# A hybrid attention and recurrent network: stick-breaking in head pairs, banded attention ahead of neighbourhood attention

## What is computed

```python
def stick_breaking_block(q_blk, k_ctx, v_ctx, q0):
    ...
    z = jnp.einsum('bthd,bshd->bhts', q_blk.astype(jnp.float32),
                   k_ctx.astype(jnp.float32)) * (SB_HEAD_DIM ** -0.5)
    before = jnp.arange(s_len)[None, :] < (q0 + jnp.arange(tq))[:, None]
    log_keep = jnp.where(before, jax.nn.log_sigmoid(-z), 0.0)
    csum = jnp.cumsum(log_keep, axis=-1)
    weights = jnp.where(before, jnp.exp(jax.nn.log_sigmoid(z) + csum[..., -1:] - csum), 0.0)
    return jnp.einsum('bhts,bshd->bthd', weights, v_ctx.astype(jnp.float32))

def stick_breaking_layer(h, norm_w, w_in, w_out):
    ...
    o = (o * jax.nn.silu(g.astype(jnp.float32))).astype(h.dtype)
    return h + o @ w_out
```

## Time and profile before

| | before |
|---|---|
| median of 3 runs | 3733.19 us (3731.39 to 3737.27) |
| profiled execution, own time | 3731.59 us |
| its span in the trace | 3729.8 us |
| mean granted clock of TensorE | 0.972 of full speed |
| PE busy | 3507.1 us (94%) |
| PE weight load busy (beside PE) | 3016.0 us (81%) |
| DVE / ACT / POOL busy | 2190.0 / 1433.8 / 720.9 us |

### The profile page before, as it was taken

One profiled execution on the slowest core, in us unless ns is written; L12 is line 12 of the kernel. 1 busy time (PEld: TensorE's weight loads), 2 busy tenths in 40 slices (PEclk: granted clock), 3 DMA queues, 4 the chain that ended last, 5 costly groups with the idle time before them and its releaser, 6 DMA issues.

```text
span 3729.8 us, 51939 instructions
## 1 busy us (share of the span) xinstructions
PE 3507.1 (94%) x19791; PEld 3016.0 (81%) x19791; DVE 2190.0 (59%) x3398; ACT 1433.8 (38%) x2512; POOL 720.9 (19%) x299
## 2 busy tenths in 40 slices
PE   6899999988999999999999898899998899899998
PEld 4899997855789999889999685778888799589656
DVE  6888885168388888778888527431226536641134
ACT  4433333147353333453333316442233623321363
POOL 1111112200211111211111230234442133033202
PEclk9999999989999999999999999999998999899999
DMA  6333332210233333333333320123332122022201
GB/s 227 103 121 124 123 114 100 63 42 1 70 129 113 113 113 119 130 121 114 119 113 100 108 74 30 46 69 101 96 101 79 41 90 85 1 74 91 62 1 57
DMA packets 94531, 333.54 MB, mean 89 GB/s; under 512 B 12273, under 2 KB 14577, under 8 KB 93425
## 3 DMA queue, kind: packets, MB, share of 16 engines
q1 hardware_dynamic: 91248, 316.28, 25.9%
q10 hardware_dynamic: 3072, 14.40, 1.0%
HBM read 322.12 MB, written 8.52 MB: 89 GB/s over the span
## 4 chain that ended last, share of the span: by engine, by line
PE 62%; issue 21%; DVE 6%; POOL 5%; ACT 3%; DMA 2%; SPq 0%; POOLq 0%; DVEq 0%; ACTq 0%
PE psum L2358 21%; PE psum L2217 16%; PE psum L2237 14%; POOL w_parts L671 5%; PE psum L2668 1%; PE psum L2684 1%; PE psum L2272 1%; PE psum L2693 1%; PE psum L2131 1%; PE psum L2460 1%; DMA mod_ring<-modw_dram 1%; DVE normed L1308 1%; PE psum L2434 0%; DVE mod_ring L1396 0%; DVE mod_products L1396 0%
## 5 line engine op out<-in xcount | busy, mean ns | idle before, releaser
L671 POOL TENSOR_TENSOR w_parts<-w_raw,w_parts 128x1024 fp32r<-128x1024 f32 x289 | 702.0, 2430 | 2903.8 <-ACT w_parts L711 2890.9
L2217 PE MATMUL psum<-h_parts,w_parts 128*128 128x264 f32 (+1 forms) x5712 | 956.7, 330 | 41.4 <-issue 13.5
L2217 PEld LDWEIGHTS psum<-h_parts,w_parts 128*128 128x128 f32 x5712 | 853.6, 190 | 139.3 <-issue 38.1
L711 ACT ACTIVATE w_parts<-w_raw 128x1024 fp32r<-128x1024 f32 x283 | 300.1, 1061 | 1134.1 <-PE psum L2217 733.8
L2237 PE MATMUL psum<-w_parts,hidden_parts 128*128 128x512 f32 x2904 | 670.7, 392 | 16.1 <-DVE hidden_parts L1268 9.5
L2237 PEld LDWEIGHTS psum<-w_parts,hidden_parts 128*128 128x128 f32 x2904 | 547.2, 189 | 135.0 <-issue 14.5
L2358 PE MATMUL psum<-h_parts,w_parts 128*128 128x384 f32 x2880 | 529.7, 335 | 18.6 <-ACT y_tok L858 14.1
L2358 PEld LDWEIGHTS psum<-h_parts,w_parts 128*128 128x128 f32 x2880 | 502.9, 188 | 23.1 <-issue 17.1
L877 ACT ACTIVATE w_parts<-psum 128x512 fp32r<-128x512 f32 x240 | 143.8, 599 | 369.6 <-PE psum L2358 140.8
L2358 PE MATMUL psum<-h_sums,w_parts 128*128 128x384 f32 x1440 | 268.9, 334 | 0.0
L2358 PEld LDWEIGHTS psum<-h_sums,w_parts 128*128 128x128 f32 x1440 | 251.3, 188 | 0.0
(11 more groups left out here) (359 smaller groups left out, 4182.7 us busy)
## 6 DMA issues: line engine op xcount, KB each, us to landing
w_raw<-wu_dram SPq DMA_DIRECT2D x295, 512.0 KB, 3.5
mod_ring<-modw_dram SPq DMA_DIRECT2D x128, 512.0 KB, 4.5
w_raw_pairs<-wg_dram SPq DMA_DIRECT2D x120, 512.0 KB, 3.7
kept_dram<-resid SPq DMA_DIRECT2D x2, 3136.0 KB, 9.9
...
```

Of the source, the lines that this page charges most:

```text
L671: pool.tensor_tensor(SPL[:, s % 2, 1], RAW[:, s % 2], SPL[:, s % 2, 0].bitcast(F32), ALU.subtract).then_inc(w_split, 1)
L711: act.activation(SPL[:, u % 2, 0], RAW[:, u % 2], ACT.Copy).then_inc(w_hi, 1)
L2217: ins = pe.matmul(PS[:, pair, PSO[a]:PSO[a] + z - a], w[:, wp, k], src[:, xp, k, t0 + a:t0 + z], start=k == 0 and n_ == 0, stop=k == KT - ...
```

## The change

**Stick-breaking in pairs.** A pair of heads is cut into three units by key tiles: tiles 2, 3 and 4 (432 columns), tile 1 (400), tile 0 (512). A unit holds both heads, in two banks, so three units are under way. The mask is written first, the score products of the two heads alternate on rows 0 to 63 and 64 to 127. DVE splits softplus into a high and a low part in fp32r, and `suffix(n, y)` subtracts part y with fp32r products of 128 rows, tile by tile; DVE's tile sums are gone. PE's order is suffix(n, 0), scores(n+2), a third of an earlier pair's values, suffix(n, 1). The gate is projected ahead of the queries, the last four query units alternate with the first scores, and the first two units of the output projection are begun before the last values.

**The mixes.** `third_fourth_high` gives a mix the `W2` tiles for its third and fourth unit, their high parts made by ACT between the two halves of `pre_apply`; PE waits for all of `v_split` only ahead of the fourth. The banded pairs come first and the neighbourhood pairs after them (the rows of the output weight are reordered on the host). The maximum is written negated, without L1697.

```diff
+SB_UNITS = 3 * 8
+SB_TILES = [(2, 3, 4), (1,), (0,)]
+SB_COLS = [432, 400, 512]
...
-            na = ot < 3
+            na = ot >= 3
+            pair = ot - 3 if na else ot
...
+            def third_fourth_high(sub):
+                u, before = sub["in"]["u"], sub["l"] + (sub["l"] > 0)
+                act.wait_ge(product_done, PRODUCTS * RUNS * (before + 1))
+                act.wait_ge(wsum_ready, 4 * RUN * RUNS * (before + 1))
+                act.wait_ge(block_low_pure, 3 * RUN * RUNS * (before + 1))
+                for j in range(2):
+                    act.wait_ge(raw_in[j], 16 * ((u + 2) // 2 + 1))
+                    act.activation(W2[j][:, 0], RAW[:, j], ACT.Copy).then_inc(w_hi, 1)
...
+                    if hi == 1 and sub["kind"] == "mix":
+                        third_fourth_high(sub)
...
-                            act.wait_ge(s_lat, 24 * mx + 4)
+                        if st["na"] and st["pair"] == 1 and st["t"] == 0:
+                            act.wait_ge(s_lat, 24 * mx + 16)
...
-                        step(dve.reduce_max(SM[:, a % 2, 0, :], sb[:, :, lo:1 + w + CTX], AX_X))
-                        dve.tensor_scalar(SM[:, a % 2, 1, :], SM[:, a % 2, 0, :], -1.0, None, ALU.mult).then_inc(s_max, 1)
+                        dve.reduce_max(SM[:, a % 2, 1, :], sb[:, :, lo:1 + w + CTX], AX_X, negate=True).then_inc(s_max, 1)
...
-                pe.wait_ge(v_split, e)
                 for j in range(2, 10):
-                    unit(u, 0, j, H, T if j in (2, 6, 7, 8) else T1, DT, [(psum_read, pr + j - 3)])
+                    if j == 3:
+                        pe.wait_ge(v_split, e)
+                    unit(u, 0, j, H, T if j in (2, 6, 7, 8) else T1, DT, [(psum_read, pr + j - 3)], w=W2[j - 2] if j < 4 else None)
...
+                def softplus_exp(n):
+                    i = n % 3
+                    t = SP[i][:, :, 0:SB_COLS[i]]
+                    act.wait_ge(z_mm, n + 1)
+                    act.activation(t, sb_both(i), ACT.Abs).then_inc(abs_ready, 1)
+                    act.wait_ge(abs_ready, n + 1)
+                    act.activation(t, t, ACT.Exp, scale=-1.0).then_inc(act_step, 1)
+                def softplus_log(n):
+                    i = n % 3
+                    t = SP[i][:, :, 0:SB_COLS[i]]
+                    act.wait_ge(act_step, 8 + n + 1)
+                    act.activation(t, t, ACT.Ln, bias=1.0).then_inc(ln_ready, 1)
+                def weights(n):
+                    m, i = n // 3, n % 3
+                    act.wait_ge(logw_mm, n + 1)
+                    if m >= 2:
+                        act.wait_ge(sb_pv, m - 1)
+                    act.activation(SW[:, m % 2, :, SB_AT[i]:SB_AT[i] + SB_COLS[i]], sb_both(i), ACT.Exp).then_inc(weight_ready, 1)
                 for j in unit_steps(u + 24, 8):
+                    if j >= 5 and j < 7:
+                        softplus_exp(j - 5)
+                        softplus_log(j - 5)
+                for n in range(SB_UNITS):
+                    if n + 2 < SB_UNITS:
+                        softplus_exp(n + 2)
+                    weights(n)
+                    if n + 2 < SB_UNITS:
+                        softplus_log(n + 2)
...
+                def softplus_sum(n):
+                    m, i = n // 3, n % 3
+                    t = SP[i]
+                    dve.wait_ge(ln_ready, n + 1)
+                    step(dve.scalar_tensor_tensor(t[:], sb_both(i), 0.0, t[:], ALU.max, ALU.add))
+                    if n >= 3:
+                        dve.wait_ge(logw_mm, 3 * m)
+                    dve.tensor_copy(sb_part(n, 0), t[:]).then_inc(sp_hi, 1)
+                    dve.wait_ge(sp_hi, n + 1)
+                    dve.tensor_tensor(sb_part(n, 1), t[:], sb_part(n, 0).bitcast(F32), ALU.subtract).then_inc(sp_low, 1)
...
+                def scores(n):
+                    m, i = n // 3, n % 3
+                    if n >= 3:
+                        pe.wait_ge(weight_ready, n - 2)
+                    for x in range(2):
+                        if i == 0:
+                            both = sb_psum(i, x, 0, 2 * SB_OFF[3]).rearrange("p (a c) -> p a c", a=2)[:, :, 0:P]
+                            pe.matmul(both, ident, mask.unsqueeze(1).broadcast_to([P, 2, P]), start=True, stop=False, skip_group_check=True)
+                            pe.matmul(sb_psum(i, x, SB_OFF[4], SB_OFF[4] + META), ident, mask[:, 0:META], start=False, stop=False,
+                                      skip_group_check=True)
+                        else:
+                            w = SB_C0[1] if i == 2 else P
+                            pe.matmul(sb_psum(i, x, 0, w), ident, mask[:, P - w:P], start=True, stop=False, skip_group_check=True)
+                    for j in SB_TILES[i]:
+                        (a, z), c0, o = SSD_TILES[j], SB_C0[j], SB_OFF[j]
+                        for x in range(2):
+                            rows = slice(x * HD, x * HD + HD)
+                            ins = pe.matmul(sb_psum(i, x, o, o + SEQ - c0, z - a), KK[rows, m, a:z], QQ[rows, m, c0:SEQ],
...
+                def suffix(n, y):
+                    m, i = n // 3, n % 3
+                    pe.wait_ge((sp_hi, sp_low)[y], n + 1)
+                    for x in range(2):
+                        own, late = sb_part(n, y)[:, x], sb_part(3 * m, y)[:, x]
+                        tile2, tile3, tile4 = late[:, 0:272], late[:, 272:416], late[:, 416:432]
+                        if i == 0:
+                            ends = sb_psum(i, x, 256, 544).rearrange("p (a c) -> p a c", a=2)[:, :, 0:META]
+                            to = [(sb_psum(i, x, 0, 432), tri, own), (sb_psum(i, x, 128, 272), minus, tile3),
+                                  (ends, minus, tile4.unsqueeze(1).broadcast_to([P, 2, META]))]
+                        elif i == 1:
+                            to = [(sb_psum(i, x, 0, 400), tri, own), (sb_psum(i, x, 128, 400), minus, tile2),
+                                  (sb_psum(i, x, 256, 400), minus, tile3), (sb_psum(i, x, 384, 400), minus, tile4)]
                         else:
-                            pe.wait_ge(sums_ready, 3 * h + 3 - j)
-                        ins = pe.matmul(sb_psum(h, j, SB_C0[j + 1], SEQ), NONES[:], sb_sum(h, j + 1), start=False, stop=True,
-                                        skip_group_check=True)
-                    ins.then_inc(logw_mm, 1)
+                            to = [(sb_psum(i, x, 0, 512), tri, own), (sb_psum(i, x, 112, 512), minus, sb_part(3 * m + 1, y)[:, x]),
+                                  (sb_psum(i, x, 240, 512), minus, tile2), (sb_psum(i, x, 368, 512), minus, tile3),
+                                  (sb_psum(i, x, 496, 512), minus, tile4)]
+                        for dst, w, part in to:
+                            ins = pe.matmul(dst, w, part, start=False, stop=y == 1, skip_group_check=True)
+                    if y == 1:
+                        ins.then_inc(logw_mm, 1)
...
+                query(4)
+                query(5)
+                pe.wait_ge(sb_const, 4)
+                pe.wait_ge(psum_read, pr + 21)
                 scores(0)
-                for h in range(HEADS + 2):
-                    if h + 1 < HEADS:
-                        scores(h + 1)
-                    if h < HEADS:
-                        suffix(h)
-                    if h >= 2 and h % 2 == 0:
-                        values(h // 2 - 1, (0, 3))
-                    if h >= 3 and h % 2 == 1:
-                        values(h // 2 - 1, (1, 2, 4))
+                query(6)
+                pe.wait_ge(psum_read, pr + 22)
+                scores(1)
+                query(7)
+                pe.wait_ge(psum_read, pr + 23)
+                for n in range(SB_UNITS):
+                    if n == 3:
+                        pe.wait_ge(psum_read, pr + 24)
+                    suffix(n, 0)
+                    if n + 2 < SB_UNITS:
+                        scores(n + 2)
+                    if n >= 3:
+                        values(n // 3 - 1, ((0,), (1,), (2, 3, 4))[n % 3])
+                    suffix(n, 1)
+                pe.wait_ge(w_split, u + 34)
+                pe.wait_ge(weight_ready, 23)
+                out_part(0, range(0, 6))
+                values(7, (0, 1, 2, 3, 4))
+                out_part(1, range(0, 6))
+                out_part(0, (6, 7))
+                out_part(1, (6, 7))
...
-        us.append(out_units_of(np.concatenate([wo[0:384], wo[384:768][pair], wo[768:]])))
+        us.append(out_units_of(np.concatenate([wo[384:768][pair], wo[0:384], wo[768:]])))
```

240 lines of the change are left out of this document (89 added, 151 removed).

## The result

The changed kernel took 3675.61 us (median of 4 runs, 3666.33 to 3679.98) against 3735.23 (4 runs); the ratio is 0.9837, 95% interval 0.9815 to 0.9860. Run once more beside the experiments it took 3671.65 (5 runs) against 3736.57, ratio 0.9833 (0.9814 to 0.9852). So it is some 60 us faster, and the 3677 of the forecast lies 1.4 us off. The profiled execution is the slowest of its four: own time 3679.98, span 3677.2.

What follows compares the result with a forecast made beforehand. PE was taken to bound stick-breaking, a round trip between PE, DVE and ACT the mixes' attention. Savings 19.8 + 13.6 + 14.5 + 8.3 = 56.2 off 3731.6 gave 3675.4, or 3677 us as median; own range 3665 to 3687, wider range 3655 to 3702.

Steps and rivals of the forecast that it cites:

- Scores overlap: Stick-breaking: two heads' score products on different row halves overlap, 2.74 us a pair of heads against 5.12.
- Rival (a): Stick-breaking: two heads' scores do not overlap and cost 5.12 a pair; 3693 us in all, chance 0.13.
- Suffix: Stick-breaking: fp32r suffix products take 7.64 us a pair instead of 8.92, with 0.14 for each product below 256 columns.
- rival (b): Stick-breaking: weight loads of 0.13 show on 24 larger suffix products, 3.1 more a pair; 3697 us, chance 0.10.
- Changes of form: Stick-breaking on PE: changes of row form, nine a pair against six or so, cost an estimated 0.6 us a pair.
- Waits: Stick-breaking: PE waits up to 0.8 us a pair for the first unit's high copy, plus 0.2 for bank reuse.
- Start and tail: Stick-breaking stage's ends: filling with queries and output products leaves 2 of 15.6 us, so 13.6 less.
- Cover: Stick-breaking: PE has 7.4 us of other work to hide the largest unit's ACT and DVE chain of 6.4 to 7.2.
- rival (d): Stick-breaking: the ACT and DVE chain outlasts its cover and each unit stands; 3759 us, slower than before, chance 0.05.
- (c): Stick-breaking: stands in each pair lower the granted clock from 1.00 to 0.90, adding 13.5; 3690 us, chance 0.09.
- Attention: Mixes' attention: dropped negation and banded pairs first give 7.6 us less in the first mix, 6.9 in the second.
- Starts of the mixes: Splits between the halves: 8.3 us less in the second mix, 0 in the first, with GpSimd's splits delaying DVE.

Runs made afterwards that it cites:

- second profile: The changed kernel itself, unaltered, run and profiled again beside the experiments: 3671.65 us, ratio 0.9833 to the kernel before; profiled span 3659.8.
- same_rows: Changed kernel with both heads' score products on rows 0 to 63: 3696.76 us, ratio 0.9897 to the kernel before.
- copy_wait: Changed kernel, the high copy of a pair's first unit waiting for the suffixes of the pair before the last: 3664.78 us, ratio 0.9814 to the kernel before.
- no_fill: Changed kernel with the last queries all ahead of the first scores and the output projection behind the last values: 3680.73 us, ratio 0.9848 to the kernel before.
- one_ahead: Changed kernel with scores made one unit ahead of the suffix instead of two: 3829.06 us, ratio 1.0243 to the kernel before.
- pool_pieces: Changed kernel with GpSimd's two splits of a mix cut into eight instructions of 128 columns each: 3672.13 us, ratio 0.9824 to the kernel before.

## Why the prediction was right

The time and the main mechanisms were right. That it came out 1.4 us off was luck: the stages gave 66.3 us instead of 56.2 (69.3 in the second profile), and executions with slower unchanged code took part of that back, 13.7 in the first profile.

- **Scores overlap: right.** 2.98 a pair against 2.74 forecast, 1.06 for the 512 columns instead of 0.95; with one set of rows 5.24 (1.91, 1.80 and 1.53). Rival (a) falls with `same_rows`.
- **Suffix: too dear by the small products.** I took 0.14 for a product below 256 columns, nearest to the mask row. One head's products of the first unit (432, 144 and 32 columns) take 0.43 (3524.00 - 3523.14, halved); less 0.20 for the large one, a small one is 0.115, below the 0.13 to 0.15 named as a sign of being right. The suffix of a pair, from the rows of the pair above, is 0.86 + 2.05 + 2.59 + 1.69 = 7.2 instead of 7.64. What it gains over float32 is read from the two traces; no run has the pairs with the old suffix. It is below the forecast, so rival (b) falls. By the rule of the Trainium skill ("TensorE: Matmul & The Clock Gate", section "LDWEIGHTS (loading the stationary operand)") a load of 128 columns takes an estimated 107 ns, nearer to the 115 ns measured for a small product than the row was. The loads' own records in this trace are longer, 189 ns on average, and overlap one another, so the trace does not show the 107 for a load by itself. The mask products still take 0.155 each, so their row is no clean price for a product between others of its own form.
- **Changes of form: a term that no run shows.** Suffix 7.2, scores 2.98, masks 1.24 and values 2.92 account for 14.33 of the 15.10, the stand for the rest. These are times from start to start, so whatever a change of form costs is in them already, and the 0.6 added beside them was one term too many.
- **Values: 0.23 too dear.** They are unchanged, but the 1.58 of the earlier trace rows holds the stand of 0.25 for ACT, so that half of a pair's values took 1.33; with the other half (3573.44 to 3575.02 in the same trace, 1.58) a pair's took 2.91 before, and 2.92 now.
- **Waits: right in kind, 0.77** instead of 1.0; `copy_wait` shows the cause. Together the pair is 15.10, not 16.2, and the steady gain 8 x 3.58 = 28.6 instead of 19.8: this is the mis-sized term, mostly by the 0.6 for changes of form and the 0.45 in the suffix.
- **Start and tail:** 40.3 - 28.6 = 11.7 against 13.6; `no_fill` gives back 13.1, of which 7.7 are PE's work at the low clock and not stands. A stand of 2.30 behind the last values was not foreseen.
- **Cover: right, and more important than priced.** In the steady pairs no unit waits for the chain of ACT and DVE, as rival (d) would have it; at the start and the end PE stands 1.09 and 0.93, and both stay when `copy_wait` moves the wait (1.09 and 0.92). The chain was put at 6.4 to 7.2; its own terms add up to 6.5 at the low end, which changes nothing. But I priced (d) by stands alone and (c) by the clock alone, as if they were two cases. `one_ahead` shows them as one: stands of 3.6 us took the clock to 0.57, and the loss doubled. So the 2.3 us a unit from which the change was to lose leaves out the clock; the point may lie lower, and where was not tried.
- **Attention: right.** Taken back alone, the order gives 5.1 and 3.7 (forecast 4.0 and 4.5) and the negation 3.1 and 2.6 (forecast 3.6 and 2.4) against the first profile; the second profile puts each 0.8 to 1.6 higher.
- **Starts of the mixes:** 10.1 instead of 8.3 in the second: the stand shrank by 8.05, as forecast, and the third unit no longer runs at a low clock behind it, which the sum left out. The first has +0.4, within what the stage varies by. The lock was told rightly from a pair of rows and is shown by `pool_pieces`: 1.4 to 1.9 in each mix.
- **What was missed:** the unchanged code. It took 13.7 more in the profiled execution, some 8 of it in the recurrent layer at clock 0.58. In the second profile it took 0.8 less than before. So it comes and goes between executions of one kernel and is not the change's doing, but it is why 66.3 us in the stages are 52.6 between the first two profiles and 60 to 65 by medians. Why the clock falls further there in one execution than in another is open.
